# Sample attention scores as three passes over split operands, in a one-core encoder-layer kernel

## What is computed

```python
q_lat = jnp.einsum('bqhd,chd->bqhc', q_nope, w_uk)
s = (jnp.einsum('bqhc,bkc->bhqk', q_lat, ckv)
     + jnp.einsum('bqhr,bkr->bhqk', q_pe, kpe)).astype(jnp.float32) * ATTN_SCALE
p = jax.nn.softmax(jnp.where(mask[None, None], s, -jnp.inf), axis=-1).astype(ckv.dtype)
o_lat = jnp.einsum('bqhk,bkc->bqhc', p, ckv)
```

## Time and profile before

| what | value |
|---|---|
| median of 3 runs | 802.61 us (801.77 to 803.9) |
| the profiled execution's own time | 802.23 us |
| its span, first to last instruction | 800.4 us |
| granted clock of TensorE, mean | 0.996 |
| busy: PE, DVE, ACT, POOL | 98%, 73%, 60%, 12% |
| share of PE in the chain that ended last | 95% |
| moved by DMA | 132.38 MB, mean 165 GB/s |

### The profile page before, as it was taken

The page is one execution under the profiler, slowest core; times in us unless marked ns, Lnnn a source line. Parts: engine busy times, 40 slices in busy tenths (PEclk is TensorE's granted clock), DMA queues, the critical chain, the costliest instruction groups (busy, mean ns, idle before and its releaser), DMA issues.

```text
span 800.4 us, 15380 instructions
## 1 busy us (share of the span) xinstructions
PE 787.9 (98%) x6175; PEld 759.8 (95%) x6175; DVE 587.9 (73%) x971; ACT 479.9 (60%) x840; POOL 96.1 (12%) x196
## 2 busy tenths in 40 slices
PE   8999999999999999999999999999999999999995
PEld 7998999999899899999999999999999999999994
DVE  5997956836845768988989887875698887655452
ACT  5893854855655678566575664444548887633432
POOL 0235112022013001111000100000000000001212
PEclk9999999999999999999999999999999999999998
DMA  8559356256346335555455544655545555555531
GB/s 305 176 181 360 106 162 209 82 159 198 117 125 194 131 108 180 156 181 158 145 174 177 178 145 137 225 158 163 165 154 173 163 158 162 174 165 159 163 128 59
DMA packets 37704, 132.38 MB, mean 165 GB/s; under 512 B 4785, under 2 KB 5697, under 8 KB 37377
## 3 DMA queue, kind: packets, MB, share of 16 engines
q1 hardware_dynamic: 31104, 109.49, 43.5%
q0 software_dynamic: 5760, 20.06, 7.8%
q10 hardware_dynamic: 768, 1.84, 0.6%
HBM read 127.17 MB, written 4.08 MB: 164 GB/s over the span
## 4 chain that ended last, share of the span: by engine, by line
PE 95%; DMA 2%; DVE 1%; ACT 1%; issue 0%; SPq 0%; ACTq 0%; DVEq 0%
PE ps_acc L453 18%; PE ps_acc L454 18%; PE ps_acc L455 18%; PE ps_row L454 3%; PE ps_row L453 3%; PE ps_row L455 3%; PE ps_tr L453 2%; PE ps_cb L454 2%; PE ps_tr L454 2%; PE ps_tr L455 2%; PE ps_cb L455 2%; PE ps_cb L453 2%; DMA wraw<-in_wst 1%; PE ps_acc L580 1%; PE ps_ss L642 1%; PE ps_s L642 1%
## 5 line engine op out<-in xcount | busy, mean ns | idle before, releaser
L1355 DVE TENSOR_TENSOR wlo<-wraw,whi 128x1024 fp32r<-128x1024 f32 x203 | 247.1, 1223 | 131.3 <-ACT whi L950 130.5
L950 ACT CAST whi<-wraw 128x1024 fp32r<-128x1024 f32 x203 | 212.1, 1046 | 133.5 <-DMA wraw<-in_wst 133.0
L453 PE MATMUL ps_acc<-xh,whi 128*128 128x288 f32 x560 | 170.8, 305 | 0.5 <-DVE mixm L1688 0.5
L454 PE MATMUL ps_acc<-xl,whi 128*128 128x288 f32 x560 | 165.2, 295 | 0.0
L455 PE MATMUL ps_acc<-xh,wlo 128*128 128x288 f32 x560 | 165.1, 295 | 0.0
L453 PEld LDWEIGHTS ps_acc<-xh,whi 128*128 128x128 f32 x560 | 105.3, 188 | 8.2 <-issue 6.9
L454 PEld LDWEIGHTS ps_acc<-xl,whi 128*128 128x128 f32 x560 | 105.4, 188 | 0.4
L455 PEld LDWEIGHTS ps_acc<-xh,wlo 128*128 128x128 f32 x560 | 105.3, 188 | 0.0
L1410 DVE SCALAR_TENSOR_TENSOR cv<-xp,vec,cv 128x292 f32<-128x292 f32 x96 | 50.1, 522 | 16.2 <-ACT cv L1012 13.9
L453 PE MATMUL ps_acc<-o_h,whi 128*128 128x288 f32 x128 | 39.1, 305 | 0.0
L454 PE MATMUL ps_acc<-o_l,whi 128*128 128x288 f32 x128 | 37.8, 295 | 0.0
(11 more groups left out here) (461 smaller groups left out, 2289.1 us busy)
## 6 DMA issues: line engine op xcount, KB each, us to landing
wraw<-in_wst SPq DMA_DIRECT2D x203, 512.0 KB, 3.5
rows<-rows_p POOLq DMA_DIRECT2D x8, 512.0 KB, 4.5
v_raw<-in_wst POOLq DMA_DIRECT2D x8, 512.0 KB, 6.2
side<-in_ukT POOLq DMA_DIRECT2D x8, 256.0 KB, 4.1
side_v<-in_ukT POOLq DMA_DIRECT2D x8, 256.0 KB, 3.8
out_ssm<-s_out POOLq DMA_DIRECT2D x8, 256.0 KB, 2.6
x<-in_xT ACTq DMA_DIRECT2D x4, 288.0 KB, 4.5
ax<-in_xT POOLq DMA_DIRECT2D x1, 1152.0 KB, 6.1
```

What stands on the lines that cost most here:

```text
L453: pe.matmul(out, w, mh, start=first, stop=False)
L454: pe.matmul(out, w, ml, start=False, stop=False)
L950: act.copy(whi[:, s % RING, :], wraw[:, s % RING, :]).then_inc(split_hi, 1)
L1355: tt(wlo[:, s % RING, :], wraw[:, s % RING, :], whi[:, s % RING, :].bitcast(F32), ALU.subtract).then_inc(split_lo, 1)
```

## The change

The sample's scores are formed as three passes. For that the latent query is split by DVE into `qlat_h` (copy out of PSUM) and `qlat_l` (subtraction), in each round, and the cache's `ckvT` is split once, in round 0: ACT makes four copies of 128 x 544 (`ckvT_h`), DVE four subtractions (`ckvT_l`, in place of `ckvT`). The tiles of the high part lie where `rows` and the convolution's output blocks of the last round lie, so `decay_rows(0)` is moved into round 3, behind that round's sample scores. On GpSimd's list the load of `cacheT` is moved ahead of `side_v_load(0)`, `cache_in` counts it alone, and the load of `cacheK` is counted on `kall_in`. The copy of the new rows counts on `kab_done`. `ssT` moves onto the place of `qlat_l`. `y_out` shares a semaphore with the second part of `misc`.

```diff
             def sample_scores(i):
-                pe.wait_ge(qlat_cp, i + 1)
+                pe.wait_ge(qlat_cp, 2 * i + 2)
                 pe.wait_ge(qz_twice, 16 * i + 16)
-                pe.wait_ge(cache_in, 32)
-                pe.wait_ge(kall_in, 32)
-                pe.wait_ge(ckt_cp, 1)
+                pe.wait_ge(kall_in, 48)
+                pe.wait_ge(cache_lo, RB)
...
                     for c in range(RB):
-                        pe.matmul(bank[:, 0:half], qlat[:, c, :], ckvT[:, c, keys], start=c == 0, stop=False)
+                        passes(bank[:, 0:half], qlat_h[:, c, :], qlat_l[:, c, :], ckvT_h(c)[:, keys],
+                               ckvT_l[:, c, keys], c == 0, False)
...
                 for c in range(2):
                     ahead(("k", i, c))
                     k_copy(i, c)
+                if i == 0:
+                    act.wait_ge(cache_in, 16)
+                    act.wait_ge(kab_done, 9)
+                    for c in range(RB):
+                        act.copy(ckvT_h(c), ckvT[:, c, :]).then_inc(cache_hi, 1)
                 fill_in(0)
...
             def qlat_copy(i):
                 dve.wait_ge(qlat_done, i + 1)
-                dve.tensor_copy(qlat[:].rearrange("p c q -> p (c q)"), ps_ss[:]).then_inc(qlat_cp, 1)
+                high = qlat_h[:].rearrange("p c q -> p (c q)")
+                dve.tensor_copy(high, ps_ss[:]).then_inc(qlat_cp, 1)
+                dve.wait_ge(qlat_cp, 2 * i + 1)
+                tt(qlat_l[:].rearrange("p c q -> p (c q)"), ps_ss[:], high.bitcast(F32), ALU.subtract
+                   ).then_inc(qlat_cp, 1)
+
+            def cache_low():
+                for c in range(RB):
+                    dve.wait_ge(cache_hi, c + 1)
+                    tt(ckvT_l[:, c, :], ckvT[:, c, :], ckvT_h(c).bitcast(F32), ALU.subtract).then_inc(cache_lo, 1)
...
                 qnat_copy(i)
                 ahead(("k", i, 1))
+                if i == 0:
+                    cache_low()
                 ahead(("x", fill(i, 0)))
                 qlat_copy(i)
...
             side_load(0)
-            side_v_load(0)
             pool.wait_ge(acum_out, 32)
             pool.dma_start(ckvT[:, :, 0:PAST], cacheT).then_inc(cache_in, 16)
-            pool.dma_start(ckvK[:, 0:4, :], cacheK).then_inc(cache_in, 16)
-            decay_rows(0)
+            side_v_load(0)
+            pool.dma_start(ckvK[:, 0:4, :], cacheK).then_inc(kall_in, 16)
...
+                    if j == 2 and i == ROUNDS - 1:
+                        pool.wait_ge(ssc_done, ROUNDS)
+                        decay_rows(0)
                     conv(fill(i, j))
```

More of the change, by code:

```diff
@@ L220, in layer_program @@
         ckvT = after("ckvT", [P, RB, KEYS])
+        ckvT_l = at("ckvT_l", [P, RB, KEYS], end[0] - RB * KEYS * 4, F32R)
         ckvK = after("ckvK", [P, 5, RANK])
@@ L254, in layer_program @@
         side_v = at("side_v", [P, 2, RANK], end[0] - 2 * RANK * 4)
-        qlat = after("qlat", [P, RB, P])
+        qlat_h = after("qlat_h", [P, RB, P], F32R)
         olat = at("olat", [P, RB, P], end[0] - RB * P * 4)
         ssc = after("ssc", [P, KEYS + P])
-        ssT = after("ssT", [P, 5, P])
+        qlat_l = after("qlat_l", [P, RB, P], F32R)
+        ssT = at("ssT", [P, 5, P], end[0] - RB * P * 4)
         stat = after("stat", [P, 4, 12])
@@ L262, in layer_program, with ckvT_h @@
         rows = after("rows", [P, HPG, SEQ])
+        ckvT_h3 = at("ckvT_h3", [P, 1, KEYS], end[0] - HPG * SEQ * 4, F32R)
+        ckvT_h0 = at("ckvT_h0", [P, 3, KEYS], Z_XC + (fill(ROUNDS - 1, 0) * CW * 4 + 31) // 32 * 32, F32R)
+        assert end[0] <= Z_XC + CB * CW * 4
+        def ckvT_h(c):
+            return ckvT_h0[:, c, :] if c < 3 else ckvT_h3[:, 0, :]
         o_h = at("o_h", [P, HEADS, T], Z_A, F32R)
@@ L337, in layer_program @@
         const_in = sem("const_in")
-        misc_in = [sem(f"misc_in{h}") for h in range(2)]
+        misc_in = [sem("misc_in"), sem("misc_y_dma")]
+        y_out = misc_in[1]
         first_in = [sem(f"first_in{p}") for p in range(PIECES)]
@@ L348, in layer_program @@
             "lat_sq", "lat_sum", "lat_std", "lat_rec", "lat_n", "lat_hi", "lat_lo")
-        ckv_out, conv_out, ck_pe, ck_cp, ckt_cp, cache_in, kall_in = sems(
-            "ckv_out", "conv_out", "ck_pe", "ck_cp", "ckt_cp", "cache_in", "kall_in")
+        ckv_out, conv_out, ck_pe, ck_cp, cache_hi, cache_lo, cache_in, kall_in = sems(
+            "ckv_out", "conv_out", "ck_pe", "ck_cp", "cache_hi", "cache_lo", "cache_in", "kall_in")
         half_done, rope_m, rope_done, qz_ready, qz_twice, qnat_done, qnat_cp, qlat_done, qlat_cp = sems(
@@ L373, in layer_program @@
             "cm_red", "cm_done", "ln1_red", "ln1_pe", "ln1_sq", "ln1_step", "ln1_std")
-        ff_step, ff_hi, ff_lo, y_ready, y_out = sems("ff_step", "ff_hi", "ff_lo", "y_ready", "y_out")
+        ff_step, ff_hi, ff_lo, y_ready = sems("ff_step", "ff_hi", "ff_lo", "y_ready")
         raw_loaded = [sem(f"raw_loaded{i}") for i in range(RING)]
@@ L441, in _ @@
                 sp.dma_start(o_y[:, 2 * q:2 * q + 2, :], d2[:, 2 * q:2 * q + 2, :]).then_inc(y_out, 16)
-            sp.wait_ge(y_out, 16 * 4)
+            sp.wait_ge(y_out, 16 * (1 + 4))
             sp.wait_ge(kpe_out, 16)
@@ L2001, in _ @@
             pool.wait_ge(kpe_out, 16)
-            pool.tensor_copy(ckvT[:, :, PAST:KEYS], ckvn[:, :, SEQ:T]).then_inc(ckt_cp, 1)
+            pool.tensor_copy(ckvT[:, :, PAST:KEYS], ckvn[:, :, SEQ:T]).then_inc(kab_done, 1)
             pool.wait_ge(lat_lo, 1)
@@ L2015, in side_v_load @@
                     pool.wait_ge(lat_lo, 2)
-                    pool.wait_ge(ckt_cp, 1)
+                    pool.wait_ge(kab_done, 9)
                     pool.wait_ge(ck_pe, 1)
```

## The result

The kernel before took 802.08 us in the same comparison (13 executions, 801.62 to 803.9), the changed kernel 804.12 us (13, 801.54 to 807.05): ratio 1.0023 [1.0015, 1.0031]. It is a little slower, where the prediction had given most of its weight to no change. The profiled execution of the changed kernel took 802.55 us (span 800.7, mean clock 0.994); the forecast was 802.4 for such an execution. So this trace shows nearly the kernel that was forecast, and the median does not. The experiments ask what the other executions have that this one lacks.

The account below looks back on a forecast made before the run. PE's own issued work was taken to bound the kernel (busy 98%). From a profiled 802.23 us, -2.7 for the passes and +2.9 for the stall gave 802.4 us; range 799.4 to 804.6.

Parts of the forecast that it names:

- The passes: PE's sample scores, each round: 24 fp32r passes at 124 ns, 2.98 us for 3.66; four rounds save 2.7 us.
- The splits: Query split on DVE each round, cache split on ACT and DVE in round 0: hidden in idle time, cost nothing.
- third rival: Splits don't fit: DVE's added 2.8 us in round 0 falls on PE, 802.3 us; counted in the forecast's 0.62.
- The order of the loads: Round 0: side_v behind ckvT lands at about 69.5 us, so PE stalls 2.9 us before q_latent.
- first rival: Round 0: side_v is served early enough, PE meets no wait, the whole gain is seen, 799.5 us; chance 0.2.
- The moved broadcast and the semaphores: decay_rows(0) in round 3, kab_done, shared y_out and ssT's new place add no unmet wait: cost nothing.
- The chance of the lower clock: The 0.18 given to round 0's stall lowering PE's clock, a loss of 2.05 us.
- second rival: Round 0's stall lowers the clock, half of 4.1 us lost, 2.05 us more: 804.5 us; chance 0.18.
- the case without a fall: The forecast itself: round 0's stall of 2.9 us with the clock held, 802.4 us; chance 0.62.
- What a measurement can tell: For the whole kernel, a change of 0.3% (2.4 us) is about the least that can be told from none.
- the lower end of the saving: PE's scores at 131 ns a pass, as for 288 columns: four rounds save only 2.0 us.
- the lower bound of the stall: PE's wait for side_v in round 0: 1.5 us in the sum's range, though nothing where the loads were priced.

Follow-up runs that it names:

- e1: The changed kernel with round 0's side_v loaded ahead of the cache again, all else kept; 800.5 us, ratio 0.9977 to the kernel before.
- e2: The kernel before, scores still plain float32, with only side_v_load(0) moved behind the load of cacheT; 806.48 us, ratio 1.0048 to the kernel before.
- e15: The kernel before, unchanged, as one more single profiled execution; 801.65 us.
- e7: e1 with DVE's sample_copy moved ahead of the next remainder; 800.73 us, ratio 0.9979 to the kernel before.
- e0: The changed kernel run once more as it is; 803.5 us, ratio 1.0020 to the kernel before; its profiled execution took 805.29 us.

## Why the prediction was right and where it failed

- **The passes: right.** 125 ns and 3.00 us a round, forecast 124 and 2.98; 0.66 to 0.69 us saved in each of rounds 1 and 2, in the profile of every kernel that has them. The estimate worked out from the gap that the Trainium skill gives (TensorE: Matmul & The Clock Gate, Back-to-back issue gap), 116 ns, was 9 ns too low.
- **The splits: right.** ACT 2.29 us (2.4), DVE 2.63 (2.8), the query's subtraction 0.69 (0.72), all of it hidden: PE has no wait at the scores. In round 1 DVE's idleness before `prob_max` is gone, as forecast, and nothing behind it became late. With e1's order the cover of DVE is gone in part and costs 0.6 us by the row, 1.2 by the length of round 0; so the third rival has its place and a price, but not in this kernel.
- **The order of the loads: right.** Stall 2.7 to 3.0 us in four profiles (2.9), `q_latent` at 69.35 to 70.28 (69.5). e2 shows it alone. `qz` landed after 5.0 us. The first rival, no stall, is refuted.
- **The moved broadcast and the semaphores: right at nothing.** No wait of PE names them.
- **The chance of the lower clock: this step failed.** The prediction had the mechanism as its second rival: a stall of 2.9 us, half speed for a while behind it, 2.05 us, 804.5 in all. It gave that 0.18 and left the term out of its sum, on the ground that the longest pause in the trace, 1.6 us, hadn't lowered the clock. That ground doesn't carry. A pause of 1.6 us says nothing for one of 2.9, and one trace shows one execution: behind that same pause, which follows one of 0.6 us closely, the last eight matmuls took 1.25 to 1.96 us in place of 1.08 in 12 of the 18 profiles of these runs, because the clock had fallen ahead of their end. e15 is one of them, and it is the same kernel. Measured in mid-kernel: at least 14 of 23 executions, by their mean clock, with 2.3 us more than the rest; 8 of them are among the 13 of the comparison, and so its median, 804.12, is one of them. The rival's price (two traces: 2.8 and 1.6 us, forecast 2.05) and the case without a fall (802.6, forecast 802.4) were near. The forecast also treated the two as alternatives for the kernel, where executions of one kernel show both.
- **What a measurement can tell: put too coarse.** The prediction took 0.3% for the least change that can be told from none. The interval of the ratio is 0.08% to either side, so the 0.23% measured are a loss clear of the noise, though below that line.
- **The range** of 799.4 to 804.6 reached into the clock case and holds the median, in part by luck: by its own numbers the lower end of the saving adds 0.7 us to 804.5, which is 805.2 and not the 804.9 that it gives, and the lower bound of the stall, 1.5 us in the sum, is worked out nowhere. Seven single executions of the 23 took more than 804.6.

**Still open.** What decides, at equal pauses of 2.7 to 3.0 us, whether the clock falls. When PE paused, as against the clock's own earlier rise, was not varied: the rise came at 6.83 and 7.55 us in the two profiles that held, at 7.63 and 5.27 in the two that didn't. Why e7, with no wait of 0.2 us or more left in round 0, gains 1.5 us and not 2.7: its profile has lost time at the start, in the late stages and at the end, which its other executions needn't share.

## What to carry to other kernels

In a kernel whose stream of matmuls waits for nobody, the order in which loads are issued is part of its schedule: ask of every load that is moved forward which smaller one now lands behind it, and who stands at the head of PE's list for that. Price a new pause in mid-kernel at its length plus a stretch at the lower clock, with a weight of a half or more at 3 us (18 of 29 executions here) and near one at 5 (11 of 11), and look at the spread and the mean clock of many executions, since one trace shows one draw. The length of an idle row is not its whole price: compare the length of the stage. If the order of the loads must stay, move work into the pause that doesn't need the late operand.

## What the hardware showed that was not expected

- The same pause of 2.7 to 3.0 us lowered the granted clock in some executions and not in others, for 3.4 us (70.1 to 73.5 in e2) or 6.8 us (69.1 to 75.9 in e0), at a cost of 1.6 and 2.8 us. The kernels whose profiles have pauses of 4.9 and 6.2 us have a mean clock of 0.992 or less in all 11 executions.
- A load on a queue of its own, issued 1.2 us later, landed after 10.1 us, where the same load at the end of a queue with 1 MB ahead of it had taken 7.7.
- The first rise of the clock lies between 5.0 and 7.9 us in the 18 profiles of these runs, and the end of round 0's keys does not follow it: 66.37 us at a rise of 4.96, 66.38 at 7.92, 67.32 at 7.81.
- PE's last eight matmuls, behind a wait of 1.6 us, take 1.08 us in some profiles and up to 1.96 in others, as the clock falls behind or ahead of them (794.14 in the kernel before, 789.46 in e7). It can cost 0.25 us in one and the same program: from their start to the end 8.90 and 8.65 us in two profiles of the changed kernel.
